# Decode softmax with each score row's own maximum, the row blocks combined by factors in the weights of the closing sum

## The reference, cut to what matters

```python
proj = rmsnorm(x) @ w_in                      # q | k | v | u
s = einsum('bqhcd,bkhcd->bhcqk', q, k)        # 4 heads, 2 score maps each (c)
p = softmax(s, axis=-1)                       # over 8192 cached positions and the new one
a = p[:, :, 0] - lam * p[:, :, 1]             # differential attention
o = einsum('bhqk,bkhe->bqhe', a, v)           # then rmsnorm over e
x = x + concat([attn, s5_mix(u)]) @ w_out
x = x + hier_moe(rmsnorm(x))                  # top-1 of 4 groups, top-2 of 8 experts
y = rmsnorm(x)
```

## Time and profile before

| | |
|---|---|
| median of 3 executions | 1459.25 us (1457.52 to 1462.02) |
| profiled execution, its own time | 1464.86 us |
| its span in the trace | 1463.1 us |
| TensorE matmuls busy | 1279.2 us, 87% of the span |
| VectorE busy | 521.6 us, 36% |
| ScalarE, GpSimd busy | 248.5 and 214.7 us, 17% and 15% |
| mean transfer rate | 313 GB/s, 458.31 MB |

### The profile page before, as it was taken

The page is one execution under the profiler, slowest core; times in us unless marked ns, Lnnn a source line. Parts: engine busy times, 40 slices in busy tenths (PEclk is TensorE's granted clock), DMA queues, the critical chain, the costliest instruction groups (busy, mean ns, idle before and its releaser), DMA issues.

```text
span 1463.1 us, 26568 instructions
## 1 busy us (share of the span) xinstructions
PE 1279.2 (87%) x9000; PEld 670.6 (46%) x9000; DVE 521.6 (36%) x1413; ACT 248.5 (17%) x476; POOL 214.7 (15%) x329
## 2 busy tenths in 40 slices
PE   7999999999869799998869999976899999999930
PEld 4545555554324346666544444433444444444410
DVE  2723543253365455553512111153122111121126
ACT  2101111121212233332212000000011111111111
POOL 2003140313100200000010000001122222222211
PEclk9999999999989999998999999976999999999975
DMA  9989998869968999999996998998899999999764
GB/s 364 329 310 293 321 294 283 272 198 298 298 227 304 352 338 363 365 315 323 331 387 228 330 336 293 322 349 321 277 324 371 360 354 363 361 363 366 256 211 179
DMA packets 185201, 458.31 MB, mean 313 GB/s; under 512 B 23953, under 2 KB 24337, under 8 KB 176530
## 3 DMA queue, kind: packets, MB, share of 16 engines
q1 hardware_dynamic: 163602, 390.21, 75.4%
q0 software_dynamic: 21504, 66.78, 13.8%
HBM read 421.92 MB, written 33.80 MB: 311 GB/s over the span
## 4 chain that ended last, share of the span: by engine, by line
PE 70%; DMA 12%; DVE 7%; SPq 5%; issue 3%; DVEq 2%; ACT 1%; POOL 0%; ACTq 0%; POOLq 0%
PE WA L1800 52%; PE SC L1800 7%; PE OD L1800 7%; DMA ring<-in_cacheK 6%; SPq L500 4%; DMA qpad<-h_scratch,idc 3%; DMA ring<-in_cacheV 2%; PE WA L2166 2%; DVE arena L1769 1%; PE WA L1919 1%; DVE arena L1782 1%; DVE st L1141 1%; PE WA L2126 1%; DMA arena<-y_scratch 1%; DVEq L1771 1%
## 5 line engine op out<-in xcount | busy, mean ns | idle before, releaser
L1800 PE MATMUL WA<-arena 128*128 128x512 f32 (+10 forms) x1440 | 353.4, 432 | 17.6 <-issue 7.2
L1800 PE MATMUL WA<-arena,xm 128*128 128x512 f32 (+3 forms) x816 | 313.6, 581 | 8.4 <-DMA arena<-in_w_out 6.5
L1800 PEld LDWEIGHTS WA<-arena 128*128 128x128 f32 (+2 forms) x1440 | 191.6, 195 | 155.0 <-issue 135.5
L1800 PEld LDWEIGHTS WA<-arena,xm 128*128 128x128 f32 (+1 forms) x816 | 124.4, 174 | 162.8 <-issue 154.7
L1800 PE MATMUL WA<-xm,arena 128*128 128x512 f32 x192 | 87.3, 603 | 1.7 <-ACT arena L958 1.3
L1800 PE MATMUL OD<-ring,sall 128*32 128x512 f32 x512 | 71.0, 670 | 15.0 <-DMA ring<-in_cacheV 15.0
L563 POOL TENSOR_TENSOR st<-st,consts 128x1 f32<-128x1 f32 (+2 forms) x18 | 13.8, 765 | 466.2 <-DVEq L1175 280.0
L1800 PE MATMUL OD<-ring,qpad 128*32 128x128 f32 x2048 | 67.9, 285 | 15.7 <-DMA ring<-in_cacheK 15.7
L1800 PEld LDWEIGHTS OD<-ring,qpad 128*32 128x32 f32 x2048 | 56.6, 114 | 35.9 <-DMA ring<-in_cacheK 18.4
L1800 PE MATMUL SC<-ring,qpad 128*32 128x128 f32 x2048 | 64.9, 278 | 9.1 <-DMA ring<-in_cacheK 9.0
L1712 DVE TENSOR_TENSOR xm<-WA,colw 128x960 f32<-128x960 f32 x16 | 18.5, 1158 | 147.2 <-PE WA L2166 147.2
(11 more groups left out here) (364 smaller groups left out, 1244.1 us busy)
## 6 DMA issues: line engine op xcount, KB each, us to landing
ring<-in_cacheK SPq DMA_DIRECT2D x512, 256.0 KB, 4.7
ring<-in_cacheV SPq DMA_DIRECT2D x512, 256.0 KB, 4.7
arena<-in_w_gu SPq DMA_DIRECT2D x16, 2048.0 KB, 9.8
arena<-in_w_dn SPq DMA_DIRECT2D x16, 1024.0 KB, 14.3
ring<-in_w_gu SPq DMA_DIRECT2D x8, 2048.0 KB, 10.3
xm<-in_w_gu SPq DMA_DIRECT2D x8, 2048.0 KB, 10.5
ring<-in_w_dn SPq DMA_DIRECT2D x8, 1024.0 KB, 14.8
xm<-in_w_dn SPq DMA_DIRECT2D x8, 1024.0 KB, 14.8
```

What stands on the lines that cost most here:

```text
L1800: return pe.matmul(out, lhsT, rhs, start=first, stop=last, **kw)
```

## The change

The exponential of each partition is taken with that partition's own maximum, so it no longer waits for the maxima of the four blocks to be brought together. The common maximum of a row is still made, but behind the first V units (m3, m4), and gives each partition a factor exp(own maximum - common maximum), which goes into the sum of the exponentials (before the product that adds the four blocks) and, with the reciprocal, into `wmap` (m4, m5). The new token's product and the maximum over the first three turns of scores are made within the last turn of K units; the exponential is taken in two halves, and the transposes of the first half may start after it; V units wait for the copies of their own turn of `sall` alone. The new token's product gets a PSUM bank from the planner. The planner's lags are set to these steps.

```diff
@@ psum_keys
+        "m1": [(("nk",) + a, 1)],
@@ streams
+                    if (t, g, y) == (TURNS - 1, 0, 1):
+                        dec.append((("m1", x), 1.0, []))
-        dec += [(("m1", x), 0.8, [(dec[-1][0], 0.9)]), (("m2", x), 0.3, [(("m1", x), 3.3)]),
-                (("m3", x), 0.3, [(("m2", x), 1.0)]), (("pt", x), 2.3, [(("m3", x), 3.2)])]
+        dec += [(("m2", x), 0.0, [(dec[-1][0], 0.6)]), (("pt", x), 2.3, [(("m2", x), 3.0)])]
+        after = {0: (("m3", x), 0.2, []), 1: (("m4", x), 0.3, [(("m3", x), 1.3)]), 2: (("m5", x), 0.3, [(("m4", x), 1.8)])}
...
-                    late = [(("pt", x), 1.2)] if t + g + y == 0 else ...
+                    late = [(("pt", x), 0.2)] if t + g + y == 0 else ...
                     dec.append((("V", x, y, t, g), 1.95, late))
+                    if y == 0 and 2 * t + g in after:
+                        dec.append(after[2 * t + g])
@@ hymba_step
-    ready = {u: ends.get(u, ends.get(u[:-1], 0.0)) + (2.4 if u[0] == "S" else 0.0) for u in PLAN}
+    lag = {"S": 2.4, "m2": 1.5, "m4": 0.7}
+    ready = {u: ends.get(u, ends.get(u[:-1], 0.0)) + lag.get(u[0], 0.0) for u in PLAN}
@@ ScalarE
+            def m2(x):
                 act.wait_ge(s_nb, x + 1)
+                for n in range(2):
+                    act.activation(sall[:, 2 * n:2 * n + 2, :], sall[:, 2 * n:2 * n + 2, :], ACT.Exp, bias=mrow[:, 1:2],
+                                   scale=HD ** -0.5, accum_out=mrow[:, 2 + 4 * n:3 + 4 * n])
+                    if n == 0:
+                        act.activation(snew[:, :], snew[:, :], ACT.Exp, bias=mrow[:, 1:2], scale=HD ** -0.5,
+                                       accum_out=mrow[:, 3:4])
+                    act.drain().then_inc(s_pexp, 1)
+            def m4(x):
+                act.wait_ge(s_md, x + 1)
+                act.activation(mrow[:, 7:8], mrow[:, 5:6], ACT.Exp, scale=HD ** -0.5).then_inc(s_mf, 1)
             def pt(x):
...
+                    act.activation(sall[:, n, :], slot("PT", x, n)[:, :], ACT.Copy).then_inc(s_ptw, 1)
@@ VectorE
             def m1(x):
...
+                dve.tensor_tensor(snew[0:32, :], slot("nk", x)[0:32, 0:NB], ..., ADD)
+                dve.drain().then_inc(free_sem("nk", x), 1)
+                dve.wait_ge(s_evac, 2 * (TURNS * x + TURNS - 1))
+                dve.reduce_max(mrow[:, 0:1], sall[:, 0:TURNS - 1, :].rearrange("p t n -> p (t n)"), AX)
+                dve.reduce_max(mrow[:, 1:2], snew[:, :], AX)
+                dve.tensor_tensor(mrow[:, 0:1], mrow[:, 0:1], mrow[:, 1:2], MAX)
+            def m2(x):
                 dve.wait_ge(s_evac, 2 * TURNS * (x + 1))
+                dve.reduce_max(mrow[:, 1:2], sall[:, TURNS - 1, :], AX)
                 dve.tensor_tensor(mrow[:, 0:1], mrow[:, 0:1], mrow[:, 1:2], MAX)
+                dve.tensor_scalar(mrow[:, 1:2], mrow[:, 0:1], -HD ** -0.5, None, MUL)
+                dve.drain().then_inc(s_nb, 1)
...
+            def m4(x):
                 dve.wait_ge(s_mb, x + 1)
+                dve.tensor_tensor(mrow[:, 5:6], mrow[:, 0:1], mbP, SUB)
+                dve.drain().then_inc(s_md, 1)
+                dve.wait_ge(s_mf, x + 1)
+                dve.tensor_tensor(mrow[:, 2:3], mrow[:, 2:3], mrow[:, 6:7], ADD)
                 dve.tensor_tensor(mrow[:, 2:3], mrow[:, 2:3], mrow[:, 3:4], ADD)
+                dve.tensor_tensor(mrow[:, 2:3], mrow[:, 2:3], mrow[:, 7:8], MUL)
                 dve.drain().then_inc(s_l, 1)
+            def m5(x):
                 dve.wait_ge(s_lP, x + 1)
                 dve.reciprocal(mrow[:, 4:5], lP)
+                dve.tensor_tensor(mrow[:, 4:5], mrow[:, 4:5], mrow[:, 7:8], MUL)
                 dve.drain().then_inc(s_l, 1)
@@ TensorE
             def m1(x):
-                pe.wait_ge(s_evac, 2 * TURNS * (x + 1))
+                vacant(pe, "nk", x)
...
+            def m3(x):
+                pe.wait_ge(s_nb, x + 1)
                 pe.transpose(mxT, mrow[:, 0:1], ident).then_inc(s_mT, 1)
+            def m4(x):
                 pe.wait_ge(s_mrep, x + 1)
                 mm(mbP, mrep[:, :, :].rearrange("a j e -> a (j e)"), ones[0:1, 0:1]).then_inc(s_mb, 1)
+            def m5(x):
+                pe.wait_ge(s_l, 2 * x + 1)
+                mm(lP, consts[:, C_SUM:C_SUM + 128], mrow[:, 2:3]).then_inc(s_lP, 1)
             def pt(x):
-                pe.wait_ge(s_pexp, x + 1)
                 for n in range(4):
+                    if n % 2 == 0:
+                        pe.wait_ge(s_pexp, 2 * x + n // 2 + 1)
...
             def Vv(x, y, r, g, p):
...
+                if y + g + p == 0:
+                    pe.wait_ge(s_ptw, 5 * x + r + 1)
```

More of the change, by code:

```diff
@@ L94, in streams @@
                 for g in range(2):
-                    late = [(("pt", x), 1.2)] if t + g + y == 0 else [(("ov", b - 2), 1.2)] if t + g == 0 and y >= 2 else []
+                    late = [(("pt", x), 0.2)] if t + g + y == 0 else [(("ov", b - 2), 1.2)] if t + g == 0 and y >= 2 else []
                     dec.append((("V", x, y, t, g), 1.95, late))
+                    if y == 0 and 2 * t + g in after:
+                        dec.append(after[2 * t + g])
                     if y and t == 0 and g == 1:
@@ L400, in hymba_step @@
         OD = ctx.enter_context(nc.psum_tensor("OD", [128, 512], f32))
[L401 removed]
+        mxT, mbP, lP = OD[0:1, 128:256], OD[:, 256:257], OD[:, 257:258]
         WA = ctx.enter_context(nc.psum_tensor("WA", [128, 512 * BANKS], f32))
@@ L424, in hymba_step @@
         s_mix = sem("s_mix")
-        s_score, s_evac, s_nk, s_m1, s_mT, s_mrep, s_mb, s_nb, s_pexp = (sem(x) for x in (
-            "s_score", "s_evac", "s_nk", "s_m1", "s_mT", "s_mrep", "s_mb", "s_nb", "s_pexp"))
+        s_score, s_evac, s_md, s_mf, s_mT, s_mrep, s_mb, s_nb, s_pexp = (sem(x) for x in (
+            "s_score", "s_evac", "s_md", "s_mf", "s_mT", "s_mrep", "s_mb", "s_nb", "s_pexp"))
         s_l, s_lP, s_ptw, s_pv, s_o4, s_aP, s_ad, s_ad2, s_dmix = (sem(x) for x in (
@@ L855, in K @@
                                ACT.Copy).then_inc(s_evac, 1)
-            def m3(x):
+            def m2(x):
                 act.wait_ge(s_nb, x + 1)
-                act.activation(sall[:, :, :], sall[:, :, :], ACT.Exp, bias=mrow[:, 1:2], scale=HD ** -0.5,
-                               accum_out=mrow[:, 2:3])
-                act.activation(snew[:, :], snew[:, :], ACT.Exp, bias=mrow[:, 1:2], scale=HD ** -0.5,
-                               accum_out=mrow[:, 3:4])
-                act.drain().then_inc(s_pexp, 1)
+                for n in range(2):
[8 more added lines that the diff above has]
+                act.activation(mrow[:, 7:8], mrow[:, 5:6], ACT.Exp, scale=HD ** -0.5).then_inc(s_mf, 1)
             def pt(x):
@@ L867, in pt @@
                     act.wait_ge(*filled("PT", x, n))
-                    act.activation(sall[:, n, :], slot("PT", x, n)[:, :], ACT.Copy)
+                    act.activation(sall[:, n, :], slot("PT", x, n)[:, :], ACT.Copy).then_inc(s_ptw, 1)
                     act.drain().then_inc(free_sem("PT", x, n), 1)
@@ L1195, in m1 @@
                 dve.tensor_tensor(mrow[:, 0:1], mrow[:, 0:1], mrow[:, 1:2], MAX)
-                dve.drain().then_inc(s_m1, 1)
+                dve.drain()
             def m2(x):
+                dve.wait_ge(s_evac, 2 * TURNS * (x + 1))
+                dve.reduce_max(mrow[:, 1:2], sall[:, TURNS - 1, :], AX)
+                dve.drain()
+                dve.tensor_tensor(mrow[:, 0:1], mrow[:, 0:1], mrow[:, 1:2], MAX)
+                dve.drain()
+                dve.tensor_scalar(mrow[:, 1:2], mrow[:, 0:1], -HD ** -0.5, None, MUL)
+                dve.drain().then_inc(s_nb, 1)
+            def m3(x):
                 dve.wait_ge(s_mT, x + 1)
@@ L1965, in m1, with m3 @@
             def m1(x):
-                pe.wait_ge(s_evac, 2 * TURNS * (x + 1))
                 if x == 0:
                     pe.wait_ge(s_qbd, 3)
+                vacant(pe, "nk", x)
                 for y in range(SPP):
                     for h in range(H):
-                        last = mm(nkP, qpad[:, h, SPP * x + y, :], knT[:, h, :], h + y == 0, h == H - 1 and y == SPP - 1)
-                last.then_inc(s_nk, 1)
-            def m2(x):
-                pe.wait_ge(s_m1, x + 1)
+                        last = mm(slot("nk", x)[0:32, 0:NB], qpad[:, h, SPP * x + y, :], knT[:, h, :], h + y == 0,
+                                  h == H - 1 and y == SPP - 1)
+                last.then_inc(full_sem("nk", x), 1)
+            def m3(x):
+                pe.wait_ge(s_nb, x + 1)
                 pe.transpose(mxT, mrow[:, 0:1], ident).then_inc(s_mT, 1)
-            def m3(x):
+            def m4(x):
                 pe.wait_ge(s_mrep, x + 1)
                 mm(mbP, mrep[:, :, :].rearrange("a j e -> a (j e)"), ones[0:1, 0:1]).then_inc(s_mb, 1)
+            def m5(x):
+                pe.wait_ge(s_l, 2 * x + 1)
+                mm(lP, consts[:, C_SUM:C_SUM + 128], mrow[:, 2:3]).then_inc(s_lP, 1)
             def pt(x):
-                pe.wait_ge(s_pexp, x + 1)
```

(4 more changed lines are left out.)

33 lines of the change are left out of this document (11 added, 22 removed).

## The result

The changed kernel takes 1488.87 us (median of 6, 1480.96 to 1495.59) against 1460.63 for the kernel before in the same session (median of 6, 1457.12 to 1466.5). The ratio is 1.0188, with a 95% interval of 1.0147 to 1.0229. (Ratios and intervals are given as they were recorded. They are not the quotients of the medians beside them, which would be 1.0193 here.) The forecast was 1456.0 with a range to 1464.5: it failed in sign and in size. The profiled execution of after took 1489.33 us, span 1487.5.

What follows compares the result with a forecast made beforehand. It took TensorE's own work in fixed order, prompt work filling the turns, as the bound. Terms -1.3 + 1.8 - 2.0 - 1.8 = -3.3 us took 1459.25 to 1456.0 us; own range 1450 to 1462, 8 in 10 within 1448 to 1464.5.

Steps and rivals of the forecast that it cites:

- a turn covered by other matmuls is worth about its idle part: Last K unit to first V unit of a pass: shortening worth -1.8 us, rather than the 18.4 us its chain shrinks.
- New operations at nothing: Added VectorE and ScalarE steps lie beside V units or filling work; uncovered, at most 1.1 us once more per pass.
- The chain behind the last K unit: Copy, last maximum and half exponential: 3.0 us until transposes may begin; half exponential released about 304.9 in the first turn.
- The page waits: TensorE's waits for pages between the two turns, 22.6 us: expected near 20, a term of -2.0 us.
- no earlier than 4 us before its present place: Sign at the first V unit: if it starts no earlier than this, the change does not do what it says.
- so I take one unit, +1.8: Between the turns: decode runs ahead of the prompt by 1.5 units, delaying the router's chain; one unit taken, +1.8 us.
- Its work up to the expert stage stays the same: TensorE up to the expert stage: same transposes and products, busy time unchanged within 2 us.
- Ends 0 and +2.7: Range in us given to the term for decode units standing before prompt work that the router's chain waits for.
- a shifted order can also put a prompt unit behind a late copy somewhere: Place not named: given, with renumbered banks, as reason for the 0.19 chance of a slower kernel.
- new-wait rival: First V units: TensorE waits 8.5 us for VectorE behind S5 scans; 1464.5 us, 1466.2 with the clock; chance 0.18.
- tail rival: End of decode: last V units leave the router's chain, first expert product some 6 us earlier; 1451.8 us; chance 0.09.
- the -1.8 for the tail: End of decode: one V unit moves from behind the routing product into the 4.11 us hole ahead; ends 0 and -5.0.

Runs made afterwards that it cites:

- e5: Changed kernel, but the planner costs the first turn as before and only the second as short: 1463.65 us, ratio 1.0027 to the kernel before.
- e7: New softmax in the old order, with weight transposes and the first two V units moved earlier in both turns: 1463.55 us, ratio 1.0042 to before.
- e1: Changed kernel's operations with TensorE's units in the order of the kernel before and the old bank numbers: 1462.26 us, ratio 0.9994 to before.
- e2: Changed kernel, same order, but the new token's product in a free corner of OD so no bank number shifts: 1487.29 us, ratio 1.0161 to before.
- e10: New softmax in the old order, with work between the last head of tiles 1, 2, 3 and their transposes moved ahead: 1486.17 us, ratio 1.0194 to before.
- e12: Changed kernel with the planner's figure between a tile's last head and its normalisation at 4.0 us instead of 3.0: 1473.96 us, ratio 1.0071 to before.
- e3: Kernel before with the planner's time for a unit's pages at 6.1 us instead of 6.0: 1473.73 us, ratio 1.0110 to before.
- e13: Changed kernel with 5, 3 and 4 matmuls that compute nothing ahead of the transposes of output tiles 1, 2, 3: 1477.72 us, ratio 1.0114 to before.
- e14: New softmax in the old order, with ten matmuls that compute nothing in the 11.1 us wait for VectorE's scan: 1462.43 us, ratio 1.0001 to before.
- e15: The ten empty matmuls in the scan wait, new softmax, old order, plus six, three and four in three other waits: 1459.91 us, ratio 0.9977 to before.
- e9: Changed kernel with q4, a V unit and a K unit moved ahead of the transposes of tiles 1, 2, 3: 1482.13 us, ratio 1.0137 to before.

## Why the prediction was wrong

**Right.** That a turn covered by other matmuls is worth about its idle part: e5 and e7 close turns and gain nothing (e7's first V unit starts at 308.64 us, forecast 308.2). New operations at nothing (e1), bank numbers (e2). The chain behind the last K unit: half of the exponential was forecast to be released 8.3 us behind it in the first turn (304.9 against 296.6), and the transposes start 8.4 us behind it (309.46 against 301.1). The page waits fell (22.6 to 15.5 us, forecast near 20). The second turn closed further than foreseen (6.8 us instead of 15), the first less (14.3 instead of 12), because a unit of 3.60 us stands ahead of its first V unit where a small one was expected. By the letter, the sign "no earlier than 4 us before its present place" came true in the profile of after (3.1 us); the turns and e2 (9.4 us) show that the change does what it says.

**The step that failed: "so I take one unit, +1.8", the term for the shifted order.** It priced the re-planned order as matmul time that has moved. Two things were wrong in it:
- The lead was three units at the fourth transpose (66 against 63), not one. The planner does not move the decode units by the 10.3 us forecast; it re-costs the turn by its own figures and interleaves anew. The order differs from that of before already from m1 on, within the last K units.
- Its price is not matmul time. "Its work up to the expert stage stays the same" holds for the instructions and fails for their durations: busy time rose by 19.2 us where I allowed 2, and idle time by 4.0. The new order left 1.9 us of work in tile 1's latency of 8.4 us, where before had 13.7. e10 shows that taking such work away ahead of tiles 1 to 3, with the lead of before and the same new softmax, costs 1.9%. In e12 most of the loss comes back while the first turn stays short (14.2 us).

**"Ends 0 and +2.7" was no bound.** It bounded the units moved, and not the waits that a changed neighbourhood opens. (The ends of the four terms add up to -16.6 and +3.4, so "by the ends of its terms" the range was 1443 to 1463 and not 1450 to 1462; the result lies outside either.) I wrote that "a shifted order can also put a prompt unit behind a late copy somewhere" and gave it no price. e3 shows what a shifted order can cost: 10.8 us for a planner figure moved by 1.7%.

**The new-wait rival** had the right mechanism, VectorE's queue ahead of TensorE, and the wrong place (the first V units: no wait of TensorE at all from 315 to 345 us) and size (8.5 us in one wait, instead of several waits of 3 to 5 us in the tiles of attention). It priced the clock once, at 1.7 us. In the profiles, longer matmuls are the larger part of the loss: 19.2 of 23.2 us against before, 26.8 of 33.8 against e1, and low-clock time rose from 113 or 92 to 159 us. That is an account of where the time went; the runs that filled waits (e13, e14, e15) did not show that filling them brings it back. The Trainium skill (TensorE: Matmul & The Clock Gate, Why this matters for your kernels) asks that no long idle gaps be left between bursts of matmuls, since the clock falls back in them. The traces agree for the gaps named here (clock at the low level for 10.2 us around the 5.1 us wait of tile 1). The prediction noted the agreement, said "every new wait" where the page speaks of longer gaps, and did not carry it into the sum.

**The tail rival** came true in its order and not in its time: the V units left the router's chain, which was itself 22 us late, and the end of decode is no shorter without them (31.7 us against 30.9). So the -1.8 for the tail was not there either.

What stays open: e10 makes the loss from waits in one stretch, but after has waits and low clock from other places too (5.3 us at the scan's product at 435, 1.8 us more from the fourth to the last tile), and no run divides the loss among them. e12 regains 1.2%; the 0.5% of e9 and the 0.7% of e13, which act at the three transposes alone, are not clear of the scatter. So it is shown that the order costs, and that waits of this kind can cost as much; how much of the 28 us they make is not.

## What to carry to other kernels

Where a planner with costs lays out a fixed order, a changed cost is a changed program: compare first a run with the new operations in the old order (e1); it says what the operations are worth. Before forecasting such an edit, look in the old order for latencies that are covered by chance (13.7 us of work where the planner asks for 3.8), since those are what a new order loses. Then look at more than the added idle time: here the matmuls became longer by as much as the idle time had grown (e10), or by four times that (after), both against e1.

## What was not expected of the hardware

In these traces waits of 5 us go with the low level of the granted clock, on an engine that is 87% busy. In after, the clock falls at 431.2 us, inside a wait of 5.3 us, and is back at 448.3. The S5 product behind the wait takes 7.86 us, where the like of it takes 4.42 at 471.29 in before, and a prompt unit takes 5.72 us at 444.03 against 3.60 at 452.03:

```profile
435.34 7.86 PE L1830 MATMUL WA<-arena 128*128 128x136 f32 x24 [5.32 <-DVEq L1180]
...
444.03 5.72 PE L1830 MATMUL WA<-arena,xm 128*128 128x512 f32 x8
...
452.03 3.60 PE L1830 MATMUL WA<-arena,xm 128*128 128x512 f32 x8
```

The scatter of one kernel goes with the clock too. The six runs of after have granted clocks of 0.922 to 0.930, and the time falls as the clock rises, from 1495.59 to 1480.96 us. Which of the two leads is not shown.
